# Modulation sums of a two-layer diffusion backbone: folded over the partitions by transfers instead of summed by TensorE

## The reference

```python
sc, scc = silu(c), silu(c_ctx)                       # 1024 numbers each: latent, context
for l in range(2):
    m  = split(sc  @ w_ada[l] + b_ada[l], 9)         # nine modulations of 1024 numbers
    mc = split(scc @ w_ada[l] + b_ada[l], 9)
    h  = h + 0.5 * m[2] * swiglu(rmsnorm(h) * (1 + m[1]) + m[0])
    ...                                              # mixing uses m[3], m[4], m[5]
    h  = h + 0.5 * m[8] * swiglu(rmsnorm(h) * (1 + m[7]) + m[6])
```

## Time and profile before

| | |
|---|---|
| median of three runs | 1578.04 us (1577.11 to 1578.14) |
| profiled execution, first to last instruction | 1575.5 us |
| the rest of the median, around that span | 2.5 us |
| TensorE matmuls busy | 1561.2 us, 99% |
| VectorE busy | 1001.6 us, 64% |
| ScalarE busy | 631.0 us, 40% |
| GpSimd busy | 82.5 us, 5% |
| TensorE's granted clock | 1.000 of full speed |

### The profile page before, as it was taken

How to read it: one execution, slowest core, us unless ns; L and a number is a source line. 1 busy time by engine, 2 the same in 40 slices (tenths; PEclk the granted TensorE clock), 3 DMA queues, 4 the chain that set the end, 5 groups by cost and what they waited for, 6 DMA issues and landing times.

```text
span 1575.5 us, 22302 instructions
## 1 busy us (share of the span) xinstructions
PE 1561.2 (99%) x9052; PEld 1338.1 (85%) x9052; DVE 1001.6 (64%) x1243; ACT 631.0 (40%) x856; POOL 82.5 (5%) x100
## 2 busy tenths in 40 slices
PE   8999999999999999999999999999999999999998
PEld 6888888888988888888888898888888897999998
DVE  5776773783967577777364267777445358975554
ACT  4433322332784343323222243333232249764553
POOL 0000000011100200000000100000000111000001
PEclk9999999999999999999999999999999999999999
DMA  9565553653322355565353336556354323456563
GB/s 365 201 197 179 186 162 119 208 192 94 115 75 79 94 166 193 176 201 173 107 196 99 107 121 201 193 183 195 100 173 148 107 91 108 147 188 197 190 203 117
DMA packets 71786, 249.95 MB, mean 159 GB/s; under 512 B 11664, under 2 KB 11920, under 8 KB 70672
## 3 DMA queue, kind: packets, MB, share of 16 engines
q1 hardware_dynamic: 71696, 248.70, 48.1%
HBM read 247.62 MB, written 1.05 MB: 158 GB/s over the span
## 4 chain that ended last, share of the span: by engine, by line
PE 96%; DVE 2%; ACT 1%; issue 0%; POOL 0%; POOLq 0%; DVEq 0%; ACTq 0%
PE bank L437 85%; PE bank L574 2%; PE bank L580 2%; PE bank L576 2%; PE bank L452 1%; PE bank L475 1%; PE bank L747 1%; PE bank L720 1%; PE bank L718 1%; PE bank L719 1%; PE bank L749 0%; PE bank L468 0%; DVE w_lo L1174 0%; PE bank L529 0%; PE bank L460 0%
## 5 line engine op out<-in xcount | busy, mean ns | idle before, releaser
L877 ACT ACTIVATE w_hi<-raw 128x1024 fp32r<-128x1024 f32 x317 | 335.9, 1060 | 807.0 <-PE bank L437 792.8
L1174 DVE TENSOR_TENSOR w_lo<-raw,w_hi 128x1024 fp32r<-128x1024 f32 x317 | 387.7, 1225 | 371.9 <-ACT w_hi L877 371.6
L437 PE MATMUL bank<-z_hi,w_hi 128*128 128x512 f32 (+1 forms) x1480 | 535.9, 362 | 2.4 <-DVE w_lo L1174 1.9
L437 PE MATMUL bank<-z_lo,w_hi 128*128 128x512 f32 (+1 forms) x1480 | 532.1, 360 | 0.0
L437 PE MATMUL bank<-z_hi,w_lo 128*128 128x512 f32 (+1 forms) x1480 | 531.9, 359 | 0.0
L437 PEld LDWEIGHTS bank<-z_hi,w_hi 128*128 128x128 f32 x1480 | 278.0, 188 | 49.7 <-DVE w_lo L1174 3.2
L437 PEld LDWEIGHTS bank<-z_hi,w_lo 128*128 128x128 f32 x1480 | 278.0, 188 | 42.6
L437 PEld LDWEIGHTS bank<-z_lo,w_hi 128*128 128x128 f32 x1480 | 278.1, 188 | 42.6 <-issue 1.0
L437 PE MATMUL bank<-h_hi,w_hi 128*128 128x512 f32 (+1 forms) x770 | 266.5, 346 | 0.0
L437 PE MATMUL bank<-h_lo,w_hi 128*128 128x512 f32 (+1 forms) x770 | 265.7, 345 | 0.0
L437 PE MATMUL bank<-h_hi,w_lo 128*128 128x512 f32 (+1 forms) x770 | 265.6, 345 | 0.0
(11 more groups left out here) (185 smaller groups left out, 1234.3 us busy)
## 6 DMA issues: line engine op xcount, KB each, us to landing
raw<-weights SPq DMA_DIRECT2D x320, 512.0 KB, 4.1
ada_raw<-ada_w SPq DMA_DIRECT2D x128, 512.0 KB, 4.2
ada_head<-head_w SPq DMA_DIRECT2D x8, 1024.0 KB, 18.5
res<-x_t SPq DMA_DIRECT2D x4, 512.0 KB, 4.8
ada_raw<-gate_w SPq DMA_DIRECT2D x4, 256.0 KB, 5.3
ws<-sgu_w SPq DMA_DIRECT2D x2, 256.0 KB, 4.0
bs<-sgu_b SPq DMA_DIRECT2D x2, 256.0 KB, 4.2
out<-final SPq DMA_DIRECT2D x2, 256.0 KB, 3.0
```

Of the source, the lines that this page charges most:

```text
L437: m = pe.matmul(bank[:, to], w, x[:, k, at], start=start and i == 0, stop=stop and i == 2, skip_group_check=True)
L877: act.activation(w_hi[:, r, :], raw[:, r, :], ACT.Copy).then_inc(hi_ready, 1)
L1174: dve.tensor_tensor(w_lo[:, r, :], raw[:, r, :], w_hi[:, r, :].bitcast(F32), ALU.subtract).then_inc(lo_ready, 1)
```

## The change

The 16 sums over partitions leave TensorE. GpSimd issues ten transfers for each modulation, inside SBUF (`fold`):

1. Two transfers that add while they write: the upper 64 partitions' first 512 outputs are added onto the lower 64, and the lower 64 partitions' last 512 outputs onto the upper 64 (256 KB each). After them each half of the partitions holds half of the outputs.
2. When both have landed, four plain transfers of 64 KB move to each group of 32 partitions its own quarter (one stream, 512 outputs) of a compact tile `ada_rows` of 128 x 512.
3. When these have landed, four adding transfers of 64 KB bring the neighbour group's share.

Then one VectorE transpose in 32 x 32 blocks (from SBUF to the accumulator, which is free by then) and one VectorE reduction over 32 columns finish the sum (`ada_turn`), and ScalarE writes the result with 16 small copies into `mods`. The turn stands in VectorE's list at slot first+8m+10, three slots after the slot of the last piece, at the latest at slot 37 of an up stage (`turn_of`); ScalarE's copies stand one slot later. `fold` stands in GpSimd's list before the preparation that needs the modulation, in the down stages behind the sums of squares of rows 1 and 4. One modulation moves from the up to the down stage in the second FFN of layer 0 and in the first of layer 1.

```diff
-UP_MODS = {(0, 0): 4, (0, 1): 4, (1, 0): 4, (1, 1): 0}
-DOWN_MODS = {(0, 0): 2, (0, 1): 1, (1, 0): 1, (1, 1): 0}
+UP_MODS = {(0, 0): 4, (0, 1): 3, (1, 0): 3, (1, 1): 0}
+DOWN_MODS = {(0, 0): 2, (0, 1): 2, (1, 0): 2, (1, 1): 0}
+TURN_LAG = 10
+TURN_BY = UP_SLOTS - 7
+FOLD_AT = (1, 4)
...
+        def turn_of(at, t):
+            for m in range(at["mods"]):
+                if t == min(at["first"] + KD * m + TURN_LAG, TURN_BY):
+                    return at["mod"] + m
+            return None
...
-            def ring_sum(at, t):
...
-                for i, mod in enumerate(full):
-                    w = acc_of(at, mod).rearrange("p s (b j i) -> p s b j i", b=KD, j=4)
-                    for st in range(2):
-                        for j in range(4):
-                            m = pe.matmul(p_ada[32 * j:32 * j + 32, i * 256:i * 256 + 256], sel[:, st, :], w[:, st, :, j, :],
-                                          start=(st == 0), stop=(st == 1), tile_position=(0, 32 * j))
-                m.then_inc(acc_read, len(full))
...
                     if mod >= 2:
-                        act.wait_ge(acc_read, mod - 1)
+                        act.wait_ge(summed, mod - 1)
...
+                mod = turn_of(at, t - 1)
+                if mod is not None:
+                    act.wait_ge(summed, mod + 1)
+                    src = ada_sums[:, mod % 2, :].rearrange("p (b j) -> p b j", j=4)
+                    for g in range(4):
+                        rows = slice(mod * KD + 4 * (g // 2), mod * KD + 4 * (g // 2) + 4)
+                        for j in range(4):
+                            act.activation(mods[32 * j:32 * j + 32, rows, g % 2], src[32 * g:32 * g + 32, :, j],
+                                           ACT.Copy).then_inc(mods_ready, 1)
...
-            def ada_turn(mod, n):
-                dve.wait_ge(mods_ready, MODS0 + mod)
-                dve.transpose(ada_turned[:, 0:n * KD, :].rearrange("p b r -> p (b r)"), p_ada[:, 0:n * 256]).then_inc(turned, n)
-                dve.wait_ge(turned, mod + n)
-                dve.tensor_copy(mods[:, mod * KD:(mod + n) * KD, :], ada_turned[:, 0:n * KD, 0:2]).then_inc(mods_ready, n)
+            def ada_turn(at, mod):
+                turned_rows = acc_of(at, mod).rearrange("p s n -> p (s n)")[:, 0:512]
+                dve.wait_ge(quarters_folded, 64 * (mod + 1))
+                dve.transpose(turned_rows, ada_rows[:]).then_inc(turned, 1)
+                dve.wait_ge(turned, mod + 1)
+                if mod >= 2:
+                    dve.wait_ge(mods_ready, MODS0 + 16 * (mod - 1))
+                dve.tensor_reduce(ada_sums[:, mod % 2, :], turned_rows.rearrange("p (b r) -> p b r", r=32),
+                                  AX_X, ALU.add).then_inc(summed, 1)
...
+            def fold(at, mod):
+                acc = acc_of(at, mod)
+                low, high = slice(0, 64), slice(64, P)
+                pool.wait_ge(acc_done, acc_count(mod, KD - 1, 1))
+                pool.dma_start(acc[low, :, 0:512], acc[high, :, 0:512], accum_op=ALU.add).then_inc(halves_folded, 16)
+                pool.dma_start(acc[high, :, 512:D], acc[low, :, 512:D], accum_op=ALU.add).then_inc(halves_folded, 16)
+                pool.wait_ge(halves_folded, 32 * (mod + 1))
+                acc = acc.rearrange("p s n -> p (s n)")
+                if mod > 0:
+                    pool.wait_ge(turned, mod)
+                for g in range(4):
+                    own = slice(32 * g, 32 * g + 32)
+                    pool.dma_start(ada_rows[own, :], acc[own, quarter(g)]).then_inc(own_moved, 16)
+                pool.wait_ge(own_moved, 64 * (mod + 1))
+                for g in range(4):
+                    own, other = slice(32 * g, 32 * g + 32), slice(32 * (g ^ 1), 32 * (g ^ 1) + 32)
+                    pool.dma_start(ada_rows[own, :], acc[other, quarter(g)], accum_op=ALU.add).then_inc(quarters_folded, 16)
...
+                    if down is not None and d in FOLD_AT[:down["mods"]]:
+                        fold(down, down["mod"] + FOLD_AT.index(d))
```

48 lines of the change are left out of this document (22 added, 26 removed).

## The result

The changed kernel takes 1611.47 us (median of 4 runs, 1610.5 to 1614.53) beside 1577.7 us for the kernel before on the same chip (4 runs, 1577.11 to 1578.14). The ratio is 1.0216, 95% interval 1.0204 to 1.0228: slower by 33.8 us. The forecast was 1561.1 us with a range up to 1582; the time lies outside, on the other side of no change.

What follows compares the result with a forecast made beforehand. TensorE was taken to bound the kernel: 1578.0 us less 16.9 for the removed sums, plus 0 for added VectorE, ScalarE and queue work, gave 1561.1 us, with 1558 to 1582 as the range holding 8 in 10.

Steps and rivals of the forecast that it cites:

- The wait that was priced at 0: VectorE's wait for a fold at each turn, 1.6 to 7.6 us, claimed to cost TensorE 0.
- F: Time of one fold from acc_done to the last landing: 16 us, range 9 to 37, gain eaten at 21.5.
- What bounds the kernel: TensorE, busy 99% with 96% of the wait chain: each microsecond off its list ends the kernel one earlier.
- What is removed: 256 summing matmuls on TensorE at line 452, in seven pairs and two singles, worth 16.9 us.
- VectorE's and ScalarE's work: Per modulation 1.4 us of transpose and reduction on VectorE, 3.2 us of copies on ScalarE; hidden beside TensorE, 0.
- What follows from F: TensorE's loss by fold time: none up to 19 us, then 16 us for every further microsecond beyond 23.
- rival 1: Folds slower than the room, TensorE stopping at up stages' second and third turns; 1602 us at F = 23, chance 0.23.
- Where VectorE meets the fold: Time from last add to turn: 14.4 us in up stages, 12.4 in down stages, 8.4 at slot 37.
- The room in a down stage: Wait at a down-stage turn that TensorE would not notice: 13 us, against 10.7 in an up stage.
- The rule weighed: VectorE holding the shared SBUF port might starve GpSimd's transfer issues: 7 us more per fold, F = 23.

Runs made afterwards that it cites:

- experiment 4: The kernel before with the 256 summing matmuls left out, so the modulations are not formed; 1559.99 us, ratio 0.9874.
- experiment 3: experiment 1 with each turn 13 slots after a modulation's first piece instead of 10 (at most 19 in down stages); 1561.80 us, ratio 0.9886.
- experiment 7: experiment 1 with the fold's first round as plain copies instead of adding transfers, same bytes and issues; 1594.27 us, ratio 1.0093.
- experiment 1: The changed kernel with 128 unused bytes behind ada_sums, so later tiles regain their old addresses modulo 256; 1613.95 us, ratio 1.0210.
- experiment 9: experiment 3 with turns after 11 slots instead of 13, the second down-stage turn still at slot 19; 1581.60 us, ratio 1.0011.
- experiment 6: experiment 1 without the fold's third round, the four adding 64 KB transfers, so modulations lack half their partial sums; 1564.68 us, ratio 0.9909.
- experiment 11: experiment 1 with late turns (13 slots, 19 at the latest) in down stages only, up stages keeping 10; 1582.13 us, ratio 1.0012.
- experiment 12: experiment 1 with late turns (13 slots) in up stages only, down stages keeping 10; 1589.43 us, ratio 1.0069.

## Why the prediction was wrong

**The step that failed, in short.** The wait that was priced at 0 costs 29.1 us of stalls: F was 21.9 us instead of 16, and in the down stages the second turn met its fold 8 us earlier, and had 4 us less room, than the prediction's sum had it. The half clock behind the stalls (10 us) and the moved tiles (11.8 us) had no term.

**What bounds the kernel: right.** TensorE's list sets the end; what was added elsewhere cost nothing until it stopped TensorE.

**What is removed: right.** 16.9 us predicted, 18.2 by time and 17.2 by span in experiment 4.

**VectorE's and ScalarE's work: right.** The reduction takes 0.69 us as assumed, the turn 1.4; busy VectorE rose by 8.3 us rather than 14. ScalarE's 256 copies take 52.5 us, 0.205 each as assumed; experiment 3 has them all and loses nothing.

**F, the first step that failed.** 16 us predicted, 22.0 at the first fold, 21.9 at the median (17.1 to 24.2). Both terms were too small. Ten issues at SP's 0.33 us made 3.3; on GpSimd's queue they take 7.4, and the steps from a signal to the next issue, priced at nothing, 0.9. The landings were 3 x 4.2 = 12.6; counted as the rows count them, from the issue's start, they are 7.82 + 6.09 + 3.33 = 17.2, and 13.7 from the end of the last issue of each round. So of the 6 us that F was off, about 4 are issues, 1 the steps between and 1 the transfers themselves. The first round, with 256 KB in each of two transfers, is the longest, and experiment 7 shows that the adding is the smaller part of it. My bounds of 9 to 37 held F; taking a value near the loads was the choice that failed. A transfer from SBUF to SBUF on a queue that had no row was priced like a load from HBM on another queue.

**What follows from F: right in part.** The prediction said "F = 20 costs 3 us in all, 21 costs 9, 22 costs 25, 23 costs 41" for the length of the stalls. At a median F of 21.9 they are 29.1 us, which fits rival 1; at 20.5 (experiment 7) they are 20.8, which doesn't fit. The prediction, and rival 1 with it, saw them at the second and third turn of each up stage; 16.9 of the 29.1 us are in down stages. Two numbers for the down stages were wrong.

**Where VectorE meets the fold, the second step that failed.** 12.4 us after the last add at both turns of a down stage, and 8.4 us at slot 37. At the first turns it was 13.0. At the second ones it was 4.6, 4.2 and 5.0 us, and 3.5 at slot 37, since the wait at the turn ahead had made the adds late and VectorE had caught up behind them. So the wait is 16.28 us where F less 12.4 would be 20.8 - 12.4 = 8.4. The prediction carried on a lateness that is left over at the next fold; here little was left over at VectorE, but the fold itself had started late.

**The room in a down stage, the third step that failed.** I gave 13 us, by the count of an up stage, slot by slot. The last row asks for three slots at once. In the changed kernel VectorE is free to take the turn at 372.7; TensorE reaches the last row at 385.6; between them must fit the wait, the turn of 1.4 and two `w_lo` of 2.35. That is 12.9 - 3.7 = 9.2 us of wait, and VectorE waited for 16.28. The stall is 16.28 - 9.2 = 7.1, and the trace shows 6.98. With a room of 13 us it would have been 16.28 - 13 = 3.3 us, and with a wait of 8.4 us none, in the measured room too. The code had this wait in plain sight; the trace of before had no stall there to point at it.

**The half clock: not in the sum.** Some 10 us. The prediction priced a stall at its length. The stall of 4.56 us cost ten longer steps behind it, 1.7 us; the one of 7.38 us 24 steps of 0.094 us more and the first one, 2.4 us.

**The placement of tiles: not in the sum, and not a rival.** 11.8 us in the span. The prediction went through instructions and waits; that a tile shrank by 128 bytes in the list of declarations is in the diff, and I read past it. Nothing in the profile of before would have shown it, since that kernel stands at the fast place.

**The rule weighed.** The prediction gave F = 23 for starving issues when VectorE holds the port. F came out near that, but the issues don't show it. In experiment 3 VectorE works on beside most folds, and the two issues of the first round take 1.92 to 2.20 us together in all 16 folds, the four of the second 2.03 to 2.06, the four of the third 3.15 to 3.20 in 15 folds (5.35 in one, as in the changed kernel); in the changed kernel, where VectorE stands idle beside the third round, they take the same. VectorE's piece operations there take 1.28 us each, and an issue that had waited for one would stand out of such narrow spreads. The issues are slow by themselves, not by waiting. Whether VectorE delays what happens between issue and landing isn't settled (experiment 3). The estimate from the Trainium skill, "DMA: Bandwidth & Descriptors", section "Anatomy of one DMA", was 8.4 us for the three rounds; from the end of their last issues they took 13.7 at the first fold, beside the weight traffic.

**The chances.** Rival 1 had 0.23 and was the mechanism. The placement isn't needed for the loss: experiment 1, without it, is slower than before by 2.1% too. A kernel with the prediction's 1561.1 us exists: experiment 3, at 1561.80. That is partly luck, since its F is 24.4 us at the median and not 16; six slots hide it where three didn't.

## What to carry to other kernels

Before work goes from a busy engine to transfers, count the whole chain of issues and landings, with rows of the same queue and direction; where there is none, put the consumer as late in its engine's list as the data allow. Lateness there cost nothing in this kernel, and earliness cost all that was queued behind (50 us, for a constant of 10 that became 13, with the tiles back in place). Where one wait delays the start of the next fold, count the second wait from the delayed start. Look for places at which the bounding engine asks for several things at once: the room there is that of the last of them. When a tile's size changes, keep the addresses of the tiles behind it, or measure the move by itself with an unused tile in the old kernel.

## What the hardware showed unexpectedly

- The place in SBUF of the tile that a product reads as its moving operand changes the time of a product of 512 columns at full clock: 0.2267 us with `h_hi` at 128 modulo 256 bytes, 0.2289 at 192, 0.2333 at 0 and at 64. At 0 that is 3% of all products that read such tiles, 10.6 us in this kernel.
- At one place in SBUF, products of 256 columns in the second FFN of layer 1 run a whole execution at 0.1133 to 0.1138 us (before, experiments 3, 4, 7 and 9) or at 0.1178 to 0.1179 (experiments 1, 6, 11 and 12), 6.6 us apart. The times of the kernel before fall in two groups with that distance: of 29 runs 21 lay at 1576.6 to 1578.2 us and 8 at 1583.5 to 1584.5. What selects the level was not found.
- An adding transfer costs GpSimd more issue than a plain one: 1.33 against 0.62 us for the second of two 256 KB ones, 0.96 against 0.63 for the first, about 1.1 against 0.52 for 64 KB. Its landing, issue included, is only 1.2 us later (8.1 against 6.9).
- TensorE came back from a stall of 4.56 us with four products at nearly the old step and then 3 us at half clock, 0.43 us a product.
